# Second-chunk key norms from the diagonal of k k^T instead of from turned tokens, in a one-core hybrid decoder block

## The chip, the cores and the metric

One core of one Trainium2 chip runs the whole program. The metric is device time in microseconds of one execution, lower is better. The kernel is written instruction by instruction for each engine: TensorE (PE), VectorE (DVE), ScalarE (ACT), GpSimd (POOL) and SyncE (SP, which only issues loads and stores).

## The reference, cut to what matters

A decoder block on x (256 tokens, 1024 channels). The input is normalised and projected by `w_in`; a gated DeltaNet branch (8 heads of 128 channels) and an attention branch (8 heads) run on parts of the projection, are gated, projected, merged and projected once more. The change touches the keys of the DeltaNet branch. They pass a causal convolution of four taps and SiLU and are normalised per token:

```python
def l2_normalize(x):
    return x * lax.rsqrt(jnp.sum(x * x, axis=-1, keepdims=True) + NORM_EPS)
...
gdiff = gc[..., :, None] - gc[..., None, :]
decay = jnp.where(tri_incl, jnp.exp(jnp.where(tri_incl, gdiff, 0.0)), 0.0)
lower = jnp.where(tri_strict, jnp.einsum('bhnid,bhnjd->bhnij', kbc, kc) * decay, 0.0)
t_mat = lax.linalg.triangular_solve(eye + lower, jnp.broadcast_to(eye, lower.shape), ...)
```

`g` is a per-token log decay and `gc` its running sum, `beta` (in `kbc`) a sigmoid; both come from 16 extra columns of the projection. The kernel takes chunks of 128 tokens, two per head (c = 0 and 1). What it needs of a token's key norm is the sum of squares over 128 channels, which is also the diagonal element of the product k k^T of that chunk.

## The kernel before, in words

**Tiles and steps.** The weights are read in tiles of 512 KB. The main loop goes over 80 of them (BRANCH0), three steps each: step S = 3n is the first third of tile n, S = 3n+1 the second, S = 3n+2 the last. A float32 product is made from rounded parts: w_hi by h_hi (first third), w_hi by h_lo (second), w_lo by h_hi (third). Every engine walks the same steps S in its own program and adds, at fixed steps, its share of the work beside the tiles; the order on each engine is written out by hand through these step numbers, and semaphores alone tie the engines together. Slots for raw, high and low parts hold 4 tiles (SLOTS); ScalarE makes the high part of tile n+2 (`split_hi`, L634) at the middle step of tile n, VectorE the low part (`split_lo`, L862) at its last step, each behind the other work of the step. SP's loads are held by s_lo: two tiles are loaded when the low part of a tile three before is done (L387).

**The first 16 tiles** are FIRST = "KVKKVKKVKKVKVVVV" (L53). K tiles give the transposed keys of one head each, into bank 0 or 1 (L1282); V tiles give the attention values in two groups of four tiles, which accumulate in two banks each (L1300; bE, bF, then bB, bE). At the end of a group `value_third` makes TensorE wait for its own last product and then adds to s_vg_p (L1306 to L1308), for which ScalarE's copies (`value_front`, L704) wait. The tiles 16 and up follow with gates, then six tiles per head, all in banks 0 and 1.

**A key head.** After K tile of head j, at three, four and six steps behind its first third: ScalarE copies the product with the first tap (L684), VectorE adds the other taps (L936), ScalarE takes tanh (L687), VectorE finishes kT_all (L949, semaphore s_kact). TensorE's `key_tokens` (L1348, steps TOKENS) turns both chunks into bank bD; ScalarE takes the sum of squares of each (L696, s_ksq) and keeps the turned first chunk (L698, s_k0). GpSimd makes the norms of two heads at once (`norms`, L474 to L483, s_sig). `similarity` on TensorE (L1359, steps SIM) makes k k^T of both chunks of head j in bank bA or bC by turns, VectorE's `similarity` (L960) multiplies it at the same step with the norm and the decay E into la_all (s_la). Before, these stand at steps 28 to 44 and the product of head j waits until head j-2 has been taken (L1354).

**Where la_all and E go.** The running sum of g (`gates`, TensorE and VectorE at S = 11, ScalarE at S = 12) is stored to memory by GpSimd as g_rows (L541), loaded back spread over the partitions (L545), masked (L495), and ScalarE takes its exponential at steps 26 to 33 (`decay`, L675). GpSimd stores la_all as blocks (L504) and loads them into `sub` (L513); from S = 58 VectorE solves the triangular systems there (`substitution`).

**The start.** TensorE turns the 8 blocks of normalised x (`turn`, L1199) into seven banks, block 7 inside the first tile (at "lh0", L1257 to L1260). ScalarE makes h_hi of each (L647), VectorE h_lo (L887). Tile 1's low part is made by VectorE in two halves (`first_lo`, L882), then the low part of the 16 gate columns (L893), for which TensorE's gate product waits at S = 4 (L1224). The product for the attention bias (L1237) is made at S = 6 in bank bB and copied by VectorE (L913).

**Banks.** Eight PSUM banks of 512 float32 columns per partition: 0 and 1, then bA to bF for 2 to 7.

```python
FIRST = "KVKKVKKVKKVKVVVV"
TOKENS = {10: 0, 16: 1, 19: 2, 24: 3, 27: 4, 32: 5, 35: 6, 40: 7}
SIM = {28: 0, 29: 1, 30: 2, 31: 3, 36: 4, 37: 5, 43: 6, 44: 7}
```

## Time and profile before

| | |
|---|---|
| median of 3 runs | 368.65 us (368.65 to 368.69) |
| the profiled execution | 368.64 us |
| its span in the trace | 366.9 us |
| TensorE busy | 357.3 us, 97% |
| VectorE busy | 269.6 us, 73% |
| ScalarE busy | 219.1 us, 60% |
| GpSimd busy | 59.7 us, 16% |
| granted TensorE clock, mean | 0.997 of full speed |

The span runs from the first to the last instruction that the profiler recorded; the device time of the same execution is 1.7 us longer. Engines are called PE, DVE, ACT, POOL and SP in the rows, and L12 is line 12 of the kernel before. In rows of a timeline or of the chain the first number is the start in us from the beginning of the span, the second the time taken in us. Rows of a timeline merge neighbouring instructions of one line (x4 is four of them), and in square brackets stands how long the engine had been idle before, and what ended it. A matmul's time in a timeline reaches until its result is out, so that neighbours overlap; the distance from start to start is what it costs the engine. A float32 product of 128 columns has two records, so a similarity of two chunks shows as x4.

### The profile page before, as it was taken

How to read it: one execution, taken by the hardware profiler on the slowest of the kernel's cores; microseconds unless marked ns; L12 is line 12 of the kernel's file. 1: busy time of each engine (PE TensorE's matmuls, PEld its weight loads, DVE VectorE, ACT ScalarE, POOL GpSimd, SP SyncE). 2: the span in 40 equal slices, each digit the busy share in tenths (PEclk: the TensorE clock that was granted, in tenths of full speed). 3: DMA queues.
4: the chain of work that ended last, by engine and by line, in shares of the span. 5: the costliest groups of instructions: out<-in, count | busy, mean ns of one | idle time of the engine just before them, and what ended most of it. 6: DMA issues, size and time to landing. Idle time of an engine off the chain costs nothing.

```text
span 366.9 us, 7653 instructions
## 1 busy us (share of the span) xinstructions
PE 357.3 (97%) x2755; PEld 343.1 (94%) x2755; DVE 269.6 (73%) x559; ACT 219.1 (60%) x500; POOL 59.7 (16%) x119
## 2 busy tenths in 40 slices
PE   7999999999999999999999999999999999999993
PEld 5889987899999999999999999999999999999882
DVE  2968876489976878978788678697885657667644
ACT  5776894455455665767676676667676542533521
POOL 1534341740033001102020202001020100000011
PEclk9999999999999999999999999999999999999998
DMA  8749549788789465544655455554456474874623
GB/s 262 204 150 283 178 124 236 185 236 226 195 198 240 114 181 152 127 117 121 178 148 129 118 134 154 142 147 117 121 151 186 118 220 134 219 230 170 236 110 114
DMA packets 99343, 62.45 MB, mean 170 GB/s; under 512 B 3652, under 2 KB 94190, under 8 KB 99310
## 3 DMA queue, kind: packets, MB, share of 16 engines
q1 hardware_dynamic: 98014, 58.59, 58.1%
q0 software_dynamic: 1296, 3.43, 3.5%
q8 instruction: 20, 0.33, 0.4%
q14 instruction: 13, 0.11, 0.1%
HBM read 60.41 MB, written 1.59 MB: 169 GB/s over the span
## 4 chain that ended last, share of the span: by engine, by line
PE 90%; DVE 3%; ACT 3%; issue 1%; DMA 1%; POOL 0%; DVEq 0%; SPq 0%; ACTq 0%; POOLq 0%
PE banks L1282 67%; PE banks L1499 6%; PE banks L1300 4%; DMA xin<-in_x_dram 1%; PE banks L1382 1%; PE banks L1389 1%; PE banks L1400 1%; ACT h_hi L647 1%; DVE w_lo L862 1%; PE banks L1438 1%; PE banks L1224 1%; PE banks L1441 1%; ACT w_hi L634 1%; DVE acc L936 1%; PE banks L1359 0%
## 5 line engine op out<-in xcount | busy, mean ns | idle before, releaser
L862 DVE TENSOR_TENSOR w_lo<-raw,w_hi 128x1024 fp32r<-128x1024 f32 x102 | 124.1, 1220 | 31.3 <-ACT w_hi L634 31.0
L634 ACT CAST w_hi<-raw 128x1024 fp32r<-128x1024 f32 x103 | 106.8, 1046 | 6.0 <-PE banks L1499 4.5
L1282 PE MATMUL banks<-h_hi,w_hi 128*128 128x256 f32 x568 | 82.3, 287 | 0.6 <-PE banks L1300 0.6
L1282 PE MATMUL banks<-h_hi,w_lo 128*128 128x256 f32 x568 | 82.4, 288 | 0.0
L1282 PE MATMUL banks<-h_lo,w_hi 128*128 128x256 f32 x568 | 82.2, 287 | 0.0
L1282 PEld LDWEIGHTS banks<-h_hi,w_hi 128*128 128x128 f32 x568 | 72.7, 191 | 2.1 <-issue 2.0
L1282 PEld LDWEIGHTS banks<-h_lo,w_hi 128*128 128x128 f32 x568 | 72.7, 191 | 0.0
L1282 PEld LDWEIGHTS banks<-h_hi,w_lo 128*128 128x128 f32 x568 | 72.7, 191 | 0.0
L936 DVE SCALAR_TENSOR_TENSOR acc<-banks,vec,acc 128x255 f32<-128x255 f32 (+2 forms) x72 | 34.5, 479 | 6.2 <-ACT acc L731 3.5
L584 POOL TENSOR_TENSOR so<-so,rnq 128x2 f32<-128x2 f32 x8 | 3.8, 471 | 148.8 <-ACT junk L798 148.8
L842 ACT CAST h_hi<-tacc 128x256 f32 x8 | 3.2, 406 | 28.4 <-DVE tacc L1163 28.4
L739 ACT ACTIVATE tz<-banks 128x256 f32<-128x256 f32 x16 | 6.1, 384 | 22.7 <-PE banks L1282 22.7
L1282 PE MATMUL banks<-y_hi,w_hi 128*128 128x256 f32 x128 | 18.0, 283 | 0.0
L1282 PE MATMUL banks<-y_hi,w_lo 128*128 128x256 f32 x128 | 18.0, 283 | 0.0
L1282 PE MATMUL banks<-y_lo,w_hi 128*128 128x256 f32 x128 | 18.0, 283 | 0.0
L731 ACT ACTIVATE acc<-banks,vec 128x256 f32<-128x256 f32 x16 | 7.6, 474 | 15.0 <-PE banks L1282 14.9
L1282 PEld LDWEIGHTS banks<-y_hi,w_hi 128*128 128x128 f32 x128 | 16.5, 192 | 0.0
L1282 PEld LDWEIGHTS banks<-y_lo,w_hi 128*128 128x128 f32 x128 | 16.5, 192 | 0.0
L1282 PEld LDWEIGHTS banks<-y_hi,w_lo 128*128 128x128 f32 x128 | 16.5, 192 | 0.0
L1499 PE MATMUL banks<-w_hi,h_hi 128*128 128x512 f32 x32 | 12.5, 389 | 0.0
L1499 PE MATMUL banks<-w_lo,h_hi 128*128 128x512 f32 x32 | 12.5, 389 | 0.0
L1499 PE MATMUL banks<-w_hi,h_lo 128*128 128x512 f32 x32 | 12.4, 389 | 0.0
(243 smaller groups left out, 544.4 us busy)
## 6 DMA issues: line engine op xcount, KB each, us to landing
raw<-in_w_in_dram SPq DMA_DIRECT2D x80, 512.0 KB, 5.1
raw<-in_w_branch_dram SPq DMA_DIRECT2D x16, 512.0 KB, 4.8
raw<-in_w_out_dram SPq DMA_DIRECT2D x8, 512.0 KB, 4.1
xin<-in_x_dram SPq DMA_DIRECT2D x2, 512.0 KB, 3.8
th_E<-g_rows POOLq DMA_DIRECT2D x2, 512.0 KB, 7.1
bias<-bias_rows POOLq DMA_DIRECT2D x1, 1024.0 KB, 6.7
raw<-in_x_dram SPq DMA_DIRECT2D x2, 512.0 KB, 3.9
out_dram<-xin SPq DMA_DIRECT2D x4, 256.0 KB, 2.0
```

The lines of the kernel that those rows point to most:

```text
L584: pool.tensor_tensor(so[:, 2:4], so[:, 0:2], rnq[:, g % 2, :], ALU.add).then_inc(s_f, 1)
L634: nc.scalar.copy(w_hi[:, t % SLOTS, :], raw[:, t % SLOTS, :]).then_inc(s_hi, 1)
L647: ac(h_hi[:, k, :], x_T[k], ACT.Copy, scale=vec[:, R_PRE + k:R_PRE + k + 1]).then_inc(s_h_hi, 1)
L731: ac(acc[:, t, :], ps, ACT.Copy, scale=tap(CONV - 1, 2 * t, h)).then_inc(s_tap0, 1)
L739: ac(tz[:, t - 4, :], ps, ACT.Tanh, scale=0.5).then_inc(s_tz, 1)
L862: v.tensor_tensor(w_lo[:, t % SLOTS, cols], raw[:, t % SLOTS, cols], w_hi[:, t % SLOTS, cols].bitcast(F32), ALU.subtract).then_inc(s_lo, 1)
L936: v.scalar_tensor_tensor(out=acc[:, a, i:], in0=ps[:, 0:SEQ - i], scalar=tap(CONV - 1 - i, w, h), in1=acc[:, a, i:], op0=ALU.mult, op1=ALU ...
L1224: last = mm(bA[0:4 * HEADS, 0:SEQ], wbd2[:, k, :], h_part[:, k, :], start=k == 0 and h_part is h_hi, stop=k == KT - 1 and h_part is h_lo)
L1282: last = mm(ps, w, r, start=part == 0 and k == 0, stop=part == 2 and k == KT - 1)
L1300: last = mm(((bE, bF), (bB, bE))[group][c], left, right, start=q == 0 and kk == 0 and part == 0, stop=q == 3 and kk == 1 and part == 2)
L1382: last = mm(bA[:, P * c:P * c + P], kT_all[:, g, P * c:P * c + P], q_T[:, P * c:P * c + P], start=True, stop=True)
L1499: last = mm(bank[2 + 2 * c + e], m[:, k, P * c:P * c + P], w[:, (OUT0 + k) % SLOTS, 512 * e:512 * e + 512], start=k == 0 and m is m_hi and ...
```

## The change

- `key_tokens`: TensorE turns only the first chunk of each head, ScalarE squares only that chunk.
- `similarity` on TensorE moves to steps 14, 16, 19, 24, 30, 32, 35 and 40. Two heads share a bank, the even one in columns 0 to 255, the odd one in columns 256 to 511. An odd head waits until VectorE has read the diagonal of the even one (s_kdiag); heads 4 and 6 wait until the pair that used the bank before has been taken; heads 0 and 2 wait until the running sums have been read from bA (s_gc).
- new on VectorE: `diagonal(j)`, one tensor_tensor_reduce of the second chunk's product with the identity, into ssqk, at the step after the product. GpSimd's `norms` waits for it as well.
- VectorE's multiplication with norm and decay stays where it was, but for heads 6 and 7, which go from steps 43, 44 to 44, 45; it waits for both products of the pair.
- the running sum's steps: 11 to 12 on TensorE and VectorE, 12 to 13 on ScalarE.
- the start: x is turned into six banks, so blocks 6 and 7 are turned inside the first tile; the bias product moves there too, into bank bC; the two small loads that it needs are issued before tile 1's; VectorE makes the gate columns' low part before the second half of tile 1's.
- TensorE no longer waits for its own product at the end of a value group; ScalarE's second copy of a group waits for the tile's semaphore.

```diff
--- before.py
+++ after.py
@@ -68,8 +68,11 @@
 U0, W0, UW_STRIDE = 99, 111, 16
 
 
+
 TOKENS = {10: 0, 16: 1, 19: 2, 24: 3, 27: 4, 32: 5, 35: 6, 40: 7}
-SIM = {28: 0, 29: 1, 30: 2, 31: 3, 36: 4, 37: 5, 43: 6, 44: 7}
+SIM = {14: 0, 16: 1, 19: 2, 24: 3, 30: 4, 32: 5, 35: 6, 40: 7}
+DIAGONAL = {15: 0, 17: 1, 20: 2, 25: 3, 31: 4, 33: 5, 36: 6, 41: 7}
+DECAYED = {28: 0, 29: 1, 30: 2, 31: 3, 36: 4, 37: 5, 44: 6, 45: 7}
 E0 = 26
 PAIRS = BLK // 2
 STEPS = 18
@@ -211,7 +214,7 @@
         tri = cst[:, C_TRI:C_TRI + P]
 
 
-        x_T = [bank[1 + k % 7][:, SEQ * (k // 7):SEQ * (k // 7) + SEQ] for k in range(KT)]
+        x_T = [bank[(1, 2, 3, 5, 6, 7)[k % 6]][:, SEQ * (k // 6):SEQ * (k // 6) + SEQ] for k in range(KT)]
 
         def tap(k, w, h):
 
@@ -281,6 +284,7 @@
         s_k0 = sem("s_k0")
         s_kact = sem("s_kact")
         s_ks_p = sem("s_ks_p")
+        s_kdiag = sem("s_kdiag")
         s_ksq = sem("s_ksq")
         s_kt_p = sem("s_kt_p")
         s_la = sem("s_la")
@@ -399,14 +403,14 @@
                     col = COL_VB + 512 * (i // 4)
                     load(n, n, w_in[256 * (i % 4):256 * (i % 4) + 256, col:col + 512].rearrange("(k p) n -> p k n", p=P))
 
-            for n in range(2):
-                first_load(n)
+            first_load(0)
+            sp.dma_start(hot, onehot).then_inc(s_hot, 16)
+            sp.dma_start(relb[0:BUCKETS, :], rel_bias).then_inc(s_hot, 16)
+            first_load(1)
             sp.dma_start(cst[:, P:], consts[:, P:]).then_inc(s_cst, 16)
             sp.dma_start(wbd[:], w_in[:, COL_BD:COL_B].rearrange("(k p) n -> p k n", p=P)).then_inc(s_bd_w, 16)
             sp.dma_start(alog[:], dn_a_log.rearrange("(a n) -> a n", a=1).to_broadcast([P, HEADS])).then_inc(s_small, 16)
             sp.dma_start(dtb[:], dn_dt_bias.rearrange("(a n) -> a n", a=1).to_broadcast([P, HEADS])).then_inc(s_small, 16)
-            sp.dma_start(hot, onehot).then_inc(s_hot, 16)
-            sp.dma_start(relb[0:BUCKETS, :], rel_bias).then_inc(s_hot, 16)
             for n in range(2, len(FIRST)):
                 first_load(n)
             for g in range(EARLY):
@@ -472,7 +476,8 @@
             def norms(q):
 
                 heads = slice(2 * q, 2 * q + 2)
-                pool.wait_ge(s_ksq, 4 * q + 4)
+                pool.wait_ge(s_ksq, 2 * q + 2)
+                pool.wait_ge(s_kdiag, 2 * q + 2)
                 pool.tensor_scalar(tk[:, 0, :, heads], ssqk[:, :, heads], 0.25, EPS, ALU.mult, ALU.add).then_inc(s_nk, 1)
                 pool.wait_ge(s_nk, 2 * q + 1)
                 pool.tensor_tensor(tk[:, 1, :, heads], tk[:, 0, :, heads], power[:, 1], ALU.pow).then_inc(s_nk, 1)
@@ -663,7 +668,7 @@
                     ac(tiny[:, 16:24], alog[:], ACT.Exp).then_inc(s_ga, 1)
                     sa.wait_ge(s_gs, 1)
                     ac(gt[:, 5], gt[:, 4], ACT.Ln).then_inc(s_ga, 1)
-                elif S == 12:
+                elif S == 13:
                     sa.wait_ge(s_gc, 3)
                     ac(tab[:, 7, :], tab[:, 5, :], ACT.Exp).then_inc(s_tab, 1)
                     ac(tab[:, 8, :], gt[:, 9, 0], ACT.Exp).then_inc(s_tab, 1)
@@ -689,18 +694,18 @@
             def key_tokens(j):
 
                 sa.wait_ge(s_kt_p, j + 1)
-                ps = bD[:, 0:256]
-                for c in range(NC):
-                    if j or c:
-                        sa.wait_ge(s_ksq, 2 * j + c)
-                    ac(junk[:, 0:P], ps[:, P * c:P * c + P], ACT.Square,
-                       accum_out=ssqk[:, c, j:j + 1]).then_inc(s_ksq, 1)
-                nc.scalar.copy(k0_all[:, j, :], ps[:, 0:P]).then_inc(s_k0, 1)
+                if j:
+                    sa.wait_ge(s_ksq, j)
+                ac(junk[:, 0:P], bD[:, 0:P], ACT.Square, accum_out=ssqk[:, 0, j:j + 1]).then_inc(s_ksq, 1)
+                nc.scalar.copy(k0_all[:, j, :], bD[:, 0:P]).then_inc(s_k0, 1)
 
             def value_front(i):
 
                 group, c = i // NC, i % NC
-                sa.wait_ge(s_vg_p, i + 1)
+                if c == 0:
+                    sa.wait_ge(s_vg_p, group + 1)
+                else:
+                    sa.wait_ge(s_tile, V_TILES[4 * group + 3] + 1)
                 nc.scalar.copy(vtok_all[:, c, 512 * group:512 * group + 512],
                                ((bE, bF), (bB, bE))[group][c]).then_inc(s_vtok, 1)
 
@@ -888,10 +893,10 @@
                                        in1=h_hi[:, k, :].bitcast(F32), op0=ALU.mult, op1=ALU.subtract).then_inc(s_h_lo, 1)
             ve.wait_ge(s_lo, 2)
             first_lo(1, 0, s_lo)
-            first_lo(1, 1, s_lo)
             ve.wait_ge(s_bd_hi, 1)
             v.tensor_tensor(wbd2[:, :, 2 * HEADS:], wbd[:], wbd2[:, :, 0:2 * HEADS].bitcast(F32),
                             ALU.subtract).then_inc(s_bd_s, 1)
+            first_lo(1, 1, s_lo)
             v.tensor_scalar(won[:], vec[:, R_ON:R_ON + 1], -0.5, None, ALU.mult).then_inc(s_vec, 1)
             v.tensor_scalar(vec_half[:], vec[:], 0.5, None, ALU.mult).then_inc(s_vec, 1)
             def gates(S):
@@ -910,7 +915,7 @@
                     for c in range(NC):
                         v.tensor_tensor(gt[:, 1, c], bd[:, c, HEADS:], dtb[:], ALU.add).then_inc(s_gv, 1)
                     ve.wait_ge(s_bias_p, 1)
-                    v.tensor_copy(brow, bB[0:HEADS, 0:BIAS_W]).then_inc(s_brow, 1)
+                    v.tensor_copy(brow, bC[0:HEADS, 0:BIAS_W]).then_inc(s_brow, 1)
                 elif S == 9:
 
                     ve.wait_ge(s_ga, 5)
@@ -920,7 +925,7 @@
                     ve.wait_ge(s_gs, 9)
                     ve.wait_ge(s_gv, 4)
                     v.tensor_tensor(tab[:, 9:11, :], gt[:, 5], gt[:, 7], ALU.add).then_inc(s_g, 2)
-                elif S == 11:
+                elif S == 12:
                     ve.wait_ge(s_gc_p, 1)
                     v.tensor_copy(grow[:], bB[0:HEADS, 0:SEQ]).then_inc(s_grow, 1)
                     v.tensor_copy(tab[:, 4:6, :], bA[:, 0:16].rearrange("p (c n) -> p c n", c=NC)).then_inc(s_gc, 1)
@@ -949,14 +954,23 @@
                     v.scalar_tensor_tensor(out=kT_all[:, j, :], in0=tacc[:, a, :], scalar=1.0, in1=acc[:, a, :],
                                            op0=ALU.add, op1=ALU.mult).then_inc(s_kact, 1)
 
+            def diagonal(j):
+
+                ve.wait_ge(s_G_p, j + 1)
+                if j:
+                    ve.wait_ge(s_kdiag, j)
+                ps = (bA, bC)[j // 2 % 2][:, 256 * (j % 2) + P:256 * (j % 2) + 2 * P]
+                v.tensor_tensor_reduce(products[:, 0:P], ps, ident, 1.0, 0.0, ALU.mult, ALU.add,
+                                       ssqk[:, 1, j:j + 1]).then_inc(s_kdiag, 1)
+
             def similarity(j):
 
                 if j % 2 == 0:
                     ve.wait_ge(s_sig, j + 1)
                 ve.wait_ge(s_E, 2 * j + 2)
-                ve.wait_ge(s_G_p, j + 1)
+                ve.wait_ge(s_G_p, j // 2 * 2 + 2)
                 for c in range(NC):
-                    ps = (bA, bC)[j % 2][:, P * c:P * c + P]
+                    ps = (bA, bC)[j // 2 % 2][:, 256 * (j % 2) + P * c:256 * (j % 2) + P * c + P]
                     v.scalar_tensor_tensor(out=la_all[:, j, c, :], in0=ps, scalar=tab[:, c, j:j + 1],
                                            in1=E_all[:, j, c, :], op0=ALU.mult, op1=ALU.mult).then_inc(s_la, 1)
 
@@ -1131,8 +1145,10 @@
                 gates(S)
                 for j in range(HEADS):
                     key_front(j, S - 3 * K_TILES[j] - 3)
-                if S in SIM:
-                    similarity(SIM[S])
+                if S in DIAGONAL:
+                    diagonal(DIAGONAL[S])
+                if S in DECAYED:
+                    similarity(DECAYED[S])
                 for g in range(HEADS):
                     stage_w(g, S - W0 - UW_STRIDE * g)
                     stage_u(g, S - U0 - UW_STRIDE * g)
@@ -1208,8 +1224,8 @@
                 turn(1, k)
             pe.wait_ge(s_pre_x0b, 1)
             pe.wait_ge(s_pre_x[1], 1)
-            for k in range(4, 7):
-                if k == 6:
+            for k in range(4, 6):
+                if k == 5:
                     pe.wait_ge(s_vec, 1)
                 for c in range(NC):
                     turn(c, k)
@@ -1231,11 +1247,7 @@
                         last = tp(bA[:, 256 + 4 * HEADS * c:256 + 4 * HEADS * (c + 1)], bd_T[:, P * c:P * c + P],
                                   ident[0:4 * HEADS, 0:4 * HEADS])
                     last.then_inc(s_bd_p, 1)
-
-                    pe.wait_ge(s_hot, 32)
-                    pe.wait_ge(s_relb, 1)
-                    mm(bB[0:HEADS, 0:BIAS_W], relb[:], hot, start=True, stop=True).then_inc(s_bias_p, 1)
-                elif S == 11:
+                elif S == 12:
 
                     pe.wait_ge(s_g, 2)
                     pe.wait_ge(s_brow, 1)
@@ -1255,9 +1267,13 @@
                 for i, which in enumerate(order):
                     k = int(which[2])
                     if which == "lh0":
-                        pe.wait_ge(s_h_lo, 1)
+                        pe.wait_ge(s_hot, 32)
+                        pe.wait_ge(s_relb, 1)
+                        mm(bC[0:HEADS, 0:BIAS_W], relb[:], hot, start=True, stop=True).then_inc(s_bias_p, 1)
+                    if which in ("lh0", "lh1"):
+                        pe.wait_ge(s_h_lo, k + 1)
                         for c in range(NC):
-                            turn(c, 7)
+                            turn(c, 6 + k)
                     if which[0] == "l":
                         pe.wait_ge(s_h_lo, k + 1)
                     else:
@@ -1303,9 +1319,6 @@
                             last.then_inc(s_vg_p, 1)
                 if part == 2:
                     last.then_inc(s_tile, 1)
-                    if q == 3:
-                        pe.wait_ge(s_tile, n + 1)
-                        pe.sem_inc(s_vg_p, 1)
 
             def bank_free(n):
 
@@ -1344,19 +1357,20 @@
                     pe.wait_ge(s_k0, j)
                 else:
                     pe.wait_ge(s_h_lo, KT)
-                for c in range(NC):
-                    last = tp(bD[:, P * c:P * c + P], kT_all[:, j, P * c:P * c + P], ident)
-                last.then_inc(s_kt_p, 1)
+                tp(bD[:, 0:P], kT_all[:, j, 0:P], ident).then_inc(s_kt_p, 1)
 
             def similarity(j):
 
-                if j >= 2:
-                    pe.wait_ge(s_la, 2 * (j - 1))
+                pe.wait_ge(s_kact, j + 1)
+                if j % 2:
+                    pe.wait_ge(s_kdiag, j)
+                elif j >= 4:
+                    pe.wait_ge(s_la, 2 * (j - 2))
                 else:
                     pe.wait_ge(s_gc, 3)
                 for c in range(NC):
-                    k = kT_all[:, j, P * c:P * c + P]
-                    last = mm((bA, bC)[j % 2][:, P * c:P * c + P], k, k, start=True, stop=True)
+                    k, col = kT_all[:, j, P * c:P * c + P], 256 * (j % 2) + P * c
+                    last = mm((bA, bC)[j // 2 % 2][:, col:col + P], k, k, start=True, stop=True)
                 last.then_inc(s_G_p, 1)
 
             def stage_a(g, s):
```

## Rows read from the trace of the kernel before

**Rows 1.** The page of the profile: busy time by engine, and the chain's shares by engine

```profile
PE 357.3 (97%) x2755; PEld 343.1 (94%) x2755; DVE 269.6 (73%) x559; ACT 219.1 (60%) x500; POOL 59.7 (16%) x119
...
PE 90%; DVE 3%; ACT 3%; issue 1%; DMA 1%; POOL 0%; DVEq 0%; SPq 0%; ACTq 0%; POOLq 0%
```

**Rows 2.** Waits of TensorE, whole span: waited for: us in total, times, longest us

```profile
PE banks L1282 <- PE banks L1300: 0.6, 2, 0.3
...
PE banks L1438 <- DVE sub L1101: 0.4, 1, 0.4
```

**Rows 3.** The chain that ended last, 14 to 112 us: start, us, what

```profile
18.68 0.74 PE banks L1237 x2
...
24.61 0.53 PE banks L1244 x4
...
30.44 0.22 PE banks L1348 x2
...
42.68 0.44 PE banks L1359 x4
...
58.42 2.76 PE banks L1300 x12
...
66.94 45.35 PE banks L1282 x376
```

**Rows 4.** Timeline of VectorE, 24 to 31 us

```profile
24.39 1.51 DVE L936 SCALAR_TENSOR_TENSOR acc<-banks,vec,acc 128x255 f32<-128x255 f32 x3
25.82 0.40 DVE L925 COPY grow<-banks 8x256 f32<-8x256 f32 x1
...
26.49 1.22 DVE L862 TENSOR_TENSOR w_lo<-raw,w_hi 128x1024 fp32r<-128x1024 f32 x1
27.63 0.42 DVE L949 SCALAR_TENSOR_TENSOR kT_all<-tacc,acc 128x256 f32<-128x256 f32 x1
...
30.89 1.23 DVE L862 TENSOR_TENSOR w_lo<-raw,w_hi 128x1024 fp32r<-128x1024 f32 x1
```

**Rows 5.** Timeline of VectorE, 42 to 55 us

```profile
42.05 1.52 DVE L936 SCALAR_TENSOR_TENSOR acc<-banks,vec,acc 128x255 f32<-128x255 f32 x3
...
44.63 0.61 DVE L960 SCALAR_TENSOR_TENSOR xin<-banks,tab,th_E 128x128 f32<-128x128 f32 x2 [0.55 <-PE banks L1359]
...
48.44 0.60 DVE L960 SCALAR_TENSOR_TENSOR xin<-banks,tab,th_E 128x128 f32<-128x128 f32 x2
...
54.05 0.99 DVE L936 SCALAR_TENSOR_TENSOR acc<-banks,vec,acc 128x255 f32<-128x255 f32 x2
```

**Rows 6.** Timeline of TensorE, 48 to 67 us

```profile
48.05 0.38 PE L1348 MATMUL banks<-cst,kT_all 128*128 128x128 f32 x2
...
57.98 0.44 PE L1348 MATMUL banks<-cst,kT_all 128*128 128x128 f32 x2 [0.44 <-DVE kT_all L949]
...
65.57 1.07 PE L1300 MATMUL banks<-w_lo,h_hi 128*128 128x512 f32 x4
```

**Rows 7.** Timeline of TensorE, 10 to 15 us

```profile
10.12 0.44 PE L1199 MATMUL banks<-cst,xin 128*128 128x128 f32 x2
...
14.60 0.30 PE L1224 MATMUL banks<-h_hi,wbd 128*32 128x256 f32 x1 [0.22 <-DVE wbd L893]
```

**Rows 8.** Timeline of ScalarE at 11.5 us: the last block of h_hi

```profile
11.49 0.52 ACT L647 ACTIVATE h_hi<-banks,vec 128x256 fp32r<-128x256 f32 x1
```

**Rows 9.** DMA traffic, 0 to 14 us in 40 slices of 0.35 us each

```profile
GB/s 0 0 0 0 0 234 140 398 421 375 398 445 386 269 315 249 218 307 328 376 357 357 392 386 310 189 77 9 37 54 156 286 323 350 345 347 309 294 288 250
```

**Rows 10.** Timeline of GpSimd at 35 us: both masks of E

```profile
35.33 2.63 POOL L495 TENSOR_SCALAR_AFFINE_SELECT th_E<-th_E 128x1024 f32<-128x1024 f32 x2 [1.46 <-DMA th_E<-g_rows]
```

**Rows 11.** Timeline of ScalarE at 40 us: the first exponentials of E

```profile
40.53 0.70 ACT L675 ACTIVATE th_E<-th_E,ng 128x128 f32<-128x128 f32 x2
```

**Rows 12.** L868 of VectorE: count, ns min/median/max, start, form

```profile
L868 DVE CUSTOM_DVE_ANT_0 bias<-xin x1: 692/692/692, 5.5 to 5.5; 128x512 f32<-128x512 f32 x1
L868 DVE DVE_READ_ACCUMULATOR2_ANT tiny<- x1: 80/80/80, 6.2 to 6.2; 128x1 f32 x1
```

## The prediction

> **What bounds the kernel now.** I read the page first. TensorE is busy 97% of the span and makes up 90% of the chain that ended last [rows 1]. So a microsecond taken off TensorE counts only where TensorE does not then wait for somebody else. The list of waits shows how little it waits: twice 0.3 us for its own matmuls at the end of a value group, and 0.4 us once late in the kernel [rows 2]. Behind 67 us it runs on, 376 matmuls in one piece [rows 3], so the question is when TensorE begins the first third of tile 16 (step S=48), today at 66.94.
>
> Next I read the stage before that in step with VectorE. VectorE works without a pause from 24.39 to past 30.89 [rows 4], and from 42.05 towards the keys of head 7 it has few gaps [rows 5]; TensorE at 57.98 waits for it [rows 6]. In this stage both engines end close together: what TensorE saves is at VectorE's mercy.
>
> **The change, part by part.**
>
> *Removed from TensorE.* Eight transposes: a pair costs 0.22 in the chain [rows 3], so 0.11 each, 0.9 in all. The wait for its own tile: the last value third starts at 65.57 and the next tile at 66.94, 1.37 us apart, while a value third costs 2.76/3 = 0.92 [rows 3, 6]. So 0.45 is lost, there and once more at tile 10. The bias product, 0.74 [rows 3], moves into the first tile, and the wait for the split gate weights (0.22 idle [rows 7]) goes because VectorE makes them half a split earlier. Total at face value: 0.9 + 0.9 + 0.7 + 0.2 = 2.7 us. I expect none of it but the last wait to survive.
>
> *First tile.* The bias product now stands between the products of block 1 and the transposes of block 6. It begins at about the 10.1 at which block 7 is turned today [rows 7]; then 0.74, a pair of turns 0.22, two matmuls at 0.12 (45.35/376 [rows 3]) and the next pair: block 7 is turned by 11.4 and visible to ScalarE about 11.6. ScalarE starts on block 7 at 11.49 today [rows 8]. I charge 0.1 us to ScalarE and to all of VectorE's work behind it. The two small loads overtake tile 1's load on SP's queue: the queue's traffic collapses to 9 GB/s in the slice at about 9.4 us, so everything issued by then, these included, has landed [rows 9], before 10.1. Tile 1's load goes out about 0.7 later and is read only after the h_hi series, so nothing.
>
> *Step 11 to 12.* VectorE's tail order becomes taps, split 5, g rows. The same work is permuted: taps to 24.39 + 1.43 = 25.82, split 1.14 to 26.96, the four small ones 0.67 (25.82 to 26.49) to 27.63 [rows 4]. All behind it stands where it did. POOL's store of g and the two loads of E start 1.1 later; POOL's mask ends at 35.33 + 2.63 = 37.96, ScalarE first reads E at 40.53, so 2.6 us cover it [rows 10, 11].
>
> *Added to VectorE.* Eight diagonals. The trace has no such instruction on 128x128 from PSUM. Lower bound: one product of that shape from PSUM, 0.30 (0.61 for two [rows 5]), and nothing for the sum. Upper bound: the 128x512 multiply-and-sum, 692 + 80 ns = 0.77 [rows 12]. The shape is that of the lower row and the extra read is that of the upper: 0.30 + 0.08, I take 0.38 of VectorE's time and 0.42 until TensorE sees it. ScalarE loses a square and its read per head; its chain is not the one below, so I book nothing. POOL's norms wait for the diagonals too: those of heads 0 to 5 are made 11, 5 and 3 steps before their first use, and the last pair decides only POOL's last store. The step of the two exponentials, the wait for vec one block sooner and ScalarE's waits for the value tiles move waits that are over by then: nothing.
>
> The Trainium skill (VectorE: DVE Perf Modes, "The TRN2 errata") gives 120 + FD cycles at 0.96 GHz for PSUM to SBUF, an estimate of 0.26 us, and its section "Two Vector instructions with no wait between them" says that an accumulator output is a second instruction. The rows of the 128x512 form agree on the second instruction, 80 ns [rows 12]; for the first, 0.30 as against 0.26, the formula would make the sum below 3 x 0.04 = 0.1 us smaller.
>
> *Added waits, the crux.* Similarity j (odd) shares a bank with j-1 and waits for diagonal j-1; the queue of tiles stands behind it.
>
> (a) S=16. The gates' g is a VectorE result and is read at about 24.6 both before and after [rows 3]; all that TensorE gained ahead of it is given back there. Gates' products about 1.1, two value thirds 1.84: TensorE is at similarity 0 at 27.5 and waits until VectorE has read the bank, 27.63 + 0.1 + 0.06 = 27.8. Then 0.44 [rows 3], a value third, a key third 0.96, one transpose: at 30.2 it stands at similarity 1. Diagonal 0 sits behind split 6 and the keys of head 2, so it begins where split 7 begins today, 30.89 [rows 4], plus 0.1, and is visible 0.42 later: similarity 1 starts at 31.45. Stall 1.2. Its tile third then starts at 31.89 against 30.44 + 0.22 = 30.66: 1.23 late.
>
> (b) S=32. Up to tile 8's end come similarities 2 and 3 (0.88) and two fewer transposes (0.22): TensorE 1.9 late. ScalarE copies tile 8's bank when it is done and VectorE's taps, today 42.05, start at 43.95. From there to diagonal 4 it has the work it has today between 42.05 and 48.44, less the 0.6 in which it waited for a similarity: 5.8 [rows 5]. So diagonal 4 starts at 49.75 and releases at 50.2. TensorE would be there at 48.05 + 1.23 - 0.33 (three single transposes instead of pairs) - 0.44 (three similarities since S=16 where there were four) + 0.11 (its transpose): 48.6. Stall 1.5.
>
> (c) S=40. After similarity 5 (0.44): value third 0.92, two key thirds 1.92, transpose and similarity 6 (0.55), key third 0.96: tile 11 ends at 55.0, the taps of head 7 start 0.5 behind, 55.5, against 54.05 [rows 5]. From them to TensorE's start at 57.98 is 3.93 today; diagonal 6 adds 0.38. TensorE gets the keys of head 7 at 59.8, 1.8 late, having waited over a microsecond.
>
> (d) The tail. From 57.98 to 66.94 is 8.96. It loses a transpose 0.11, similarity 6 0.44 (done earlier) and the wait for its own tile 0.45: 7.96. Tile 16 starts at 67.76, **0.8 us later**.
>
> Sum: the profiled execution took 368.64 us (span 366.9), the median of the runs is 368.65, so the two are one number. 368.64 + 0.8 = **369.45**, slower by 0.22%, just over the 0.2% that a measurement of this kernel can tell from no change. Behind 67 us no instruction is added; POOL's last store of blocks comes some 1.5 us later, and the substitution with it, but TensorE's only late wait of 0.4 us [rows 2] shows that this path is off its back. The cover is VectorE's room there; if it is used up, the late products of head 0 wait by what is left.
>
> **Rivals.**
>
> *Faster: VectorE reaches diagonals 0 and 4 in time.* Then (a) and (b) vanish. Place: S=16 and S=32. Point: diagonal 0 would have to be out by 30.2, 1.2 us sooner than 31.4. TensorE would be 2.6 us further on at tile 11, ahead of today, but the taps of head 7 then wait for VectorE's and ScalarE's own work, which is today's: they start near today's 54.05, earlier by what ScalarE's missing square gives, and diagonal 6 takes that back. The keys come at today's 57.98, and with the tail of 7.96 tile 16 starts at 65.94: 1.0 less, **367.65**. For it: VectorE has idle time before 42. Against it: none of it lies in the stretch from 24.39 to 30.89.
>
> *No change.* The stalls are there, but a diagonal costs the lower bound, 0.30, without the read, and the first tile costs ScalarE nothing: three diagonals lie on the chain (0, 4, 6), 3 x 0.1 less, and 0.1: 369.05, 0.1% over today. Within 0.2% too is anything up to 369.38.
>
> *Slower by more.* The diagonal costs the upper bound: 3 x 0.37 more, **370.55**. Or the first tile delays ScalarE by more than 0.1: each tenth comes through whole.
>
> *Not what it says: TensorE's wait at the value groups stays in another form*, since tile 16's bank or its weights hold it: 0.45 on the tail, 369.9. Against it: the list has that wait twice only, behind tiles 10 and 15 [rows 2].
>
> The change's own wait cannot be a matter of chance: the Trainium skill (PSUM — Partial Sum Buffer, "PSUM bank collisions raise a hardware error") says that a write by TensorE and a read by VectorE in one bank collide even at different columns. No row here shows such an overlap; without the wait the time would be the first rival's.
>
> **How the numbers follow.** Forecast with its own spread (369.4 to 369.9): 0.45. No change by cheap diagonals or by VectorE a few tenths ahead: 0.33. Faster: 0.12. Dearer diagonals or a late first tile: 0.10. Slower by over 0.2% takes the last and, with the wait that stays, nearly all of the first: 0.54; within 0.2% 0.34; faster 0.12. The range 367.9 to 370.5 takes in all but the full first rival and the far end of the upper bound.
>
> **What the profile after would show.** TensorE idle at similarity 1 (about 1.2 us, near 31) and at similarity 5 (about 1.4, near 50), both released by VectorE's new line, about 1.2 us at the last key transpose, near 59; no idle at tile 16, which starts near 67.7; diagonals of 0.30 plus a read of 0.08. Wrong if similarity 1 starts without a wait, if a diagonal takes over 0.6, or if the start of tile 16 and the end differ in their shift.

## The result, and the profile after

| | before, same chips | after |
|---|---|---|
| median of the runs | 368.69 us (6 runs, 368.65 to 369.06) | 372.28 us (6 runs, 371.64 to 372.77) |
| ratio | 1 | 1.0095 [1.0084, 1.0105] |
| profiled execution | 368.64 us | 372.37 us |
| its span | 366.9 us | 370.6 us |
| granted TensorE clock, mean | 0.997 | 0.995 |

The change costs 3.6 us where 0.8 was forecast, and the time lies outside the range given. The clock has no part in it: 0.995 as against 0.997 of full speed, the higher of the two levels (2.4 GHz) in both.

I read the page first, the line of busy times and the chain's shares, columns as in [rows 1].

```profile
PE 356.9 (96%) x2747; PEld 342.1 (92%) x2747; DVE 271.2 (73%) x575; ACT 216.9 (59%) x484; POOL 60.3 (16%) x119
...
PE 74%; DVE 12%; DMA 6%; issue 4%; ACT 2%; POOL 2%; DVEq 0%; SPq 0%; POOLq 0%; ACTq 0%
```

TensorE is busy 0.4 us less than before and the program takes 3.7 us more. Its share of the chain falls from 90% to 74%, and transfers, which had 1%, now have 6%. So the end is now set in part by a way that leads through transfers and VectorE. The list of TensorE's waits (us in total, times, longest) says what stops it:

```profile
PE banks L1373 <- DVE ssqk L963: 1.7, 2, 0.9
PE banks L1298 <- DVE acc L941: 1.5, 1, 1.5
...
PE banks L1360 <- DVE kT_all L954: 1.0, 1, 1.0
PE banks L1298 <- DVE w_lo L867: 0.5, 1, 0.5
```

The first line is the similarities' wait for the diagonals (two of them), the third the wait for the keys of head 7: both forecast. The second and the fourth were not, and the wait of the value groups in [rows 2] is gone.

**Up to tile 16.** TensorE between 30 and 69 us (start, us, idle before in brackets):

```profile
30.59 0.27 PE L1360 MATMUL banks<-cst,kT_all 128*128 128x128 f32 x1
31.62 0.68 PE L1373 MATMUL banks<-kT_all 128*128 128x128 f32 x4 [0.76 <-DVE ssqk L963]
...
47.07 0.68 PE L1373 MATMUL banks<-kT_all 128*128 128x128 f32 x4 [0.27 <-DVE xin L974]
...
49.45 0.27 PE L1360 MATMUL banks<-cst,kT_all 128*128 128x128 f32 x1
50.63 0.68 PE L1373 MATMUL banks<-kT_all 128*128 128x128 f32 x4 [0.92 <-DVE ssqk L963]
...
60.37 0.33 PE L1360 MATMUL banks<-cst,kT_all 128*128 128x128 f32 x1 [1.05 <-DVE kT_all L954]
...
67.36 1.07 PE L1316 MATMUL banks<-w_lo,h_hi 128*128 128x512 f32 x4
68.27 1.11 PE L1298 MATMUL banks<-h_hi,w_hi 128*128 128x256 f32 x8
```

Similarity 1 starts at 31.62 and similarity 5 at 50.63 (forecast 31.45 and 50.2), head 7's keys are turned at 60.37 (59.8), and tile 16 follows its forerunner by 0.91 us without an idle moment, at 68.27 instead of 66.94 [rows 3]: **1.33 us late**, where I had 0.82. VectorE's diagonal is two instructions, as expected:

```profile
31.19 0.28 DVE L963 CUSTOM_DVE_ANT_0 sub<-banks,cst 128x128 f32<-128x128 f32 x1
31.40 0.08 DVE L963 DVE_READ_ACCUMULATOR2_ANT ssqk<- 128x1 f32 x1
```

0.28 and 0.08, where I took 0.30 and 0.08. The estimate of 0.26 worked out from the Trainium skill (VectorE: DVE Perf Modes, "The TRN2 errata") is 0.02 under the row, and the second instruction is there, as the Trainium skill's section "Two Vector instructions with no wait between them" on the same page says.

**Behind tile 16.** The span is 3.7 us longer and tile 16 only 1.33 late: the other 2.4 us are lost behind 67 us, where the change adds no instruction. The chain that ended last (start, us, what), followed back from the stop of TensorE at 110.97, shows by which way:

```profile
64.39 0.33 DVE xin L974
64.72 1.05 DVE w_lo L867
65.77 0.61 DVE xin L974 x2
...
66.94 0.65 POOL m_blocks L509
...
68.76 5.35 DMA m_blocks<-xin
...
74.39 0.48 POOL sub L518
74.87 6.54 DMA sub<-m_blocks
...
81.56 0.10 DVE sub L989
...
83.95 1.22 DVE w_lo L867
...
102.48 4.67 DMA raw<-in_w_in_dram
107.17 1.06 ACT w_hi L639
...
110.97 5.06 PE banks L1298 x40
```

Read from the top: VectorE's decay product of head 6, a low part of weights, the product of head 7, GpSimd's store of the blocks, its landing, the load of `sub`, its landing, and the substitution. There VectorE stands still with its weight work queued behind. The same three places in the timelines of VectorE and GpSimd, first before, then after:

```profile
64.28 2.40 POOL L504 DMA_DIRECT2D m_blocks<-xin  x4 [3.10 <-DVE xin L960]
...
70.24 0.97 POOL L513 DMA_DIRECT2D sub<-m_blocks  x2 [2.56 <-DMA m_blocks<-xin]
...
75.61 0.09 DVE L975 MEMSET sub<- 128x32 f32 x1
```

```profile
66.94 2.41 POOL L509 DMA_DIRECT2D m_blocks<-xin  x4 [2.59 <-DVE xin L974]
...
74.39 0.97 POOL L518 DMA_DIRECT2D sub<-m_blocks  x2 [4.03 <-DMA m_blocks<-xin]
...
81.56 0.09 DVE L989 MEMSET sub<- 128x32 f32 x1 [4.67 <-DMA sub<-m_blocks]
```

The store goes out 2.66 us later, the load 4.15 later, the substitution starts 5.95 later, and 4.67 of that VectorE spends idle.

Part of the 2.66 lies in the norms of heads 6 and 7, for which VectorE's product of head 6 waits (it starts at 64.11), and which now wait for the diagonal of head 7. GpSimd's first instruction of these norms, before and after:

```profile
59.31 0.19 POOL L476 TENSOR_SCALAR tk<-ssqk 128x4 f32<-128x4 f32 x1 [4.27 <-ACT junk L696]
```

```profile
61.65 1.02 POOL L481 TENSOR_SCALAR tk<-ssqk 128x4 f32<-128x4 f32 x1 [3.31 <-DVE ssqk L963]
```

It is not only later but takes 0.8 us longer, beside a low part that VectorE makes from 61.40 to 62.62, and it lies on the chain. No run isolates these 0.8 us.

From 66 to 126 us the list of waits then shows ScalarE, which splits the weights, short of them; before, that wait was 0.4 us in all:

```profile
ACT w_hi L639 <- DMA raw<-in_w_in_dram: 14.5, 9, 3.2
```

SP may load two tiles only when a low part is done, the low parts stand behind the idle VectorE, so the loads come late in a row. TensorE uses up its lead and stops before 85.22 (0.48 us) and 110.97 (1.49 us). Its weight loads, listed apart from its matmuls, wait 0.7 and 1.7 us at these two places, together the 2.4.

### The profile page after: what moved, and what is told of

Read it like the earlier page. It is cut to its first block, busy times and chain, and to the rows that moved or that the text cites. A ratio compares the mean times of both kernels' runs of the same rounds, so it can differ in the third digit from the quotient of the medians.

```text
span 370.6 us, 7651 instructions
## 1 busy us (share of the span) xinstructions
PE 356.9 (96%) x2747; PEld 342.1 (92%) x2747; DVE 271.2 (73%) x575; ACT 216.9 (59%) x484; POOL 60.3 (16%) x119
## 4 chain that ended last, share of the span: by engine, by line
PE 74%; DVE 12%; DMA 6%; issue 4%; ACT 2%; POOL 2%; DVEq 0%; SPq 0%; POOLq 0%; ACTq 0%
PE banks L1298 54%; PE banks L1513 6%; DVE w_lo L867 5%; DVE acc L941 2%; DMA sub<-m_blocks 2%; DVE sub L1014 1%; DMA m_blocks<-xin 1%; DMA raw<-in_w_in_dram 1%; DMA xin<-in_x_dram 1%; PE banks L1316 1%; PE banks L1396 1%; PE banks L1403 1%; PE banks L1414 1%; DVE xin L974 1%; PE banks L1373 1%
```

## The experiments

The question was how the 3.6 us divide between the stage before tile 16 and the way of the blocks behind it, which edit pays for each, and which part was lost in a third way. Each expectation names its theories in its own words. Edits are against the kernel before (the `before` diffs) or the changed kernel (`after`).

**Late blocks alone, in the kernel before.** VectorE's product of head 7 goes from step 44 to 48, TensorE's stays.

```diff
--- before
+DVE_SIM = {28: 0, 29: 1, 30: 2, 31: 3, 36: 4, 37: 5, 43: 6, 48: 7}
...
-                if S in SIM:
-                    similarity(SIM[S])
+                if S in DVE_SIM:
+                    similarity(DVE_SIM[S])
```

> The kernel before with one multiplication of VectorE (norm and decay of head 7) moved from step 44 to step 48, nothing else. Theory 1 (the second half of the loss is the blocks' way: la of head 7, GpSimd's last store of blocks, its load, VectorE's substitution, the weight splits queued behind it): the last store is issued some 2.4 us later (near 66.7 instead of 64.28), VectorE waits for the blocks at step 58 for 3 to 5 us, TensorE's tile 16 still starts at 66.94, and the kernel loses 1.5 to 2.5 us: 370.2 to 371.2. Theory 2 (the loss behind tile 16 has another cause, such as the loads of E or the norms being late): within 0.3 us of before, 368.4 to 369.0.

Measured: 368.82 us, ratio 1.0001 [0.9992, 1.0011]: nothing. The run missed its own condition: VectorE reaches step 48 early, so the store went out at 65.76, only 1.48 later. What it does show is that a delay of this size is free; the substitution started at 76.51 after 0.84 us of idle VectorE, and nobody felt it.

**Later blocks, in the kernel before.** The same with step 50, and behind ScalarE's copy of the last values.

```diff
--- before
+DVE_SIM = {28: 0, 29: 1, 30: 2, 31: 3, 36: 4, 37: 5, 43: 6, 50: 7}
...
+                if j == 7:
+                    ve.wait_ge(s_vtok, 4)
```

> The kernel before with VectorE's multiplication for head 7 at step 50 and behind ScalarE's last copy of the values, so that GpSimd's last store of blocks goes out near 68.3 us, 4 us later than before and 1.4 us later than in the changed kernel. Theory 1 (the blocks' way costs nothing up to a threshold between the 1.5 us of the run with step 48 and the changed kernel's 2.7, and then everything): VectorE waits over 3 us at the substitution with a weight split behind it, the loads of weights come late, TensorE waits for splits or taps, and the kernel loses 1 to 3 us, 369.8 to 371.8, though TensorE starts tile 16 at 66.9. Theory 2 (lateness of the blocks is harmless and the changed kernel lost behind tile 16 by something else): 368.4 to 369.2.

Measured: 370.09 us, ratio 1.0036 [1.0022, 1.0049]. The store went out at 69.04, 4.76 later than before and later than meant; it landed fast (a median of 1.9 us), so that the substitution starts only 3.94 later, 2.0 earlier than in the changed kernel. The timeline of VectorE has, with the changed kernel's signature:

```profile
79.55 0.09 DVE L978 MEMSET sub<- 128x32 f32 x1 [3.60 <-DMA sub<-m_blocks]
```

and its list of waits, 66 to 126 us:

```profile
ACT w_hi L635 <- DMA raw<-in_w_in_dram: 12.7, 10, 2.7
...
PE banks L1285 <- DVE acc L937: 0.8, 1, 0.8
```

Its profiled execution took 370.34 us, 1.7 over that of before: 0.3 arose before tile 16 (67.25), 1.4 behind it. So late blocks cost time by themselves, without one diagonal in the kernel, though not the whole 2.4 us, since they come less late.

**The decay products of heads 6 and 7 at their old steps.**

```diff
--- after
-DECAYED = {28: 0, 29: 1, 30: 2, 31: 3, 36: 4, 37: 5, 44: 6, 45: 7}
+DECAYED = {28: 0, 29: 1, 30: 2, 31: 3, 36: 4, 37: 5, 43: 6, 44: 7}
```

> The changed kernel with the decay products of heads 6 and 7 at steps 43 and 44 as before, so that no weight split stands between them. Theory 1: the last store of blocks goes out 1.1 us earlier (near 65.8), the wait at the substitution shrinks by 1 to 3 us, tile 16 stays at 68.3, and 0.5 to 2 us come back: 370.3 to 371.8. Theory 2: unchanged, 372.0 to 372.6.

Measured: 369.92 us (369.85 to 370.02), ratio 1.0032 [1.0020, 1.0044]: **2.4 us back from two step numbers**, more than the first theory gave (370.3 at best). VectorE and GpSimd:

```profile
64.12 1.13 DVE L974 SCALAR_TENSOR_TENSOR xin<-banks,tab,th_E 128x128 f32<-128x128 f32 x4 [1.49 <-POOL tab L485]
...
76.89 0.09 DVE L989 MEMSET sub<- 128x32 f32 x1
```

```profile
65.81 2.40 POOL L509 DMA_DIRECT2D m_blocks<-xin  x4 [1.46 <-DVE xin L974]
...
71.66 0.97 POOL L518 DMA_DIRECT2D sub<-m_blocks  x2 [2.44 <-DMA m_blocks<-xin]
```

Without the split of weights between the two products (they ran at 64.11 and 65.77) the store is 1.13 us earlier, but the load is 2.73 earlier and the substitution 4.67. Tile 16 starts at 68.28, as in the changed kernel, and TensorE has no wait at all between 66 and 126 us. What is left, 369.92 against 368.73 before, is 1.2 us: tile 16's 1.33.

**The substitution five steps later.** If VectorE's idle stand at 81.56 is the harm, putting the substitution where its data are there should avert it.

```diff
--- after
-SUB_AT = [58, 59, 59, 61, 62, 64, 65, 67, 68, 70, 73, 73, 74, 76, 77, 79, 81, 82]
+SUB_AT = [s + 5 for s in [58, 59, 59, 61, 62, 64, 65, 67, 68, 70, 73, 73, 74, 76, 77, 79, 81, 82]]
```

> The changed kernel with all 18 steps of VectorE's substitution five steps later, nothing else. Theory 1: the blocks come as late as in the changed kernel, but VectorE no longer stands at them with the weight splits behind it; the two late waits of TensorE (0.5 us for a split, 1.5 us for the taps) go, tile 16 stays at 68.3, so 370.2 to 370.4, 1.9 us under the changed kernel. Theory 2 (the substitution's end is what counts, through the loads of the solved blocks for step 99): the same as the changed kernel or slower, 372 to 374.

Measured: 373.5 us (373.26 to 374.93), 1.2 over the changed kernel. The substitution starts at 82.70 without idling, but the solved blocks are stored at 109.33 instead of 107.13 (before 101.66), and TensorE waits for them:

```profile
PE banks L1431 <- issue: 2.3, 1, 2.3
```

The list names no releaser. By the program this product waits for VectorE's turn of the blocks that GpSimd has loaded back, and VectorE's timeline has it just before TensorE goes on at 123.18:

```profile
122.64 0.45 DVE L1086 STREAM_TRANSPOSE sub<-T_all 128x256 f32<-128x256 f32 x1 [3.72 <-DMA T_all<-t_blocks]
```

The blocks' way has a deadline at its far end too, as the second theory had it. Moving the wait did not help; bringing the blocks earlier, in the run with the old steps, did.

**Diagonals 0 and 4 one step earlier.** The first then stands ahead of the weight split of step 14, the other ahead of a tap and two decay products.

```diff
--- after
-DIAGONAL = {15: 0, 17: 1, 20: 2, 25: 3, 31: 4, 33: 5, 36: 6, 41: 7}
+DIAGONAL = {14: 0, 17: 1, 20: 2, 25: 3, 30: 4, 33: 5, 36: 6, 41: 7}
```

> The changed kernel with two of VectorE's diagonals one step earlier: head 0 at step 14, ahead of the low part of tile 6, and head 4 at step 30, ahead of the decay product of head 2. Theory 1 (the waits of TensorE for diagonals 0 and 4 make the loss before tile 16): both waits fall under 0.3 us, the keys of head 7 come about 1.5 us earlier, tile 16 starts at 66.5 to 66.9, GpSimd's last store is issued about 1.5 us earlier, and the kernel comes to 368.2 to 369.6. Theory 2 (VectorE is the bound anyway and gives the time back elsewhere): tile 16 stays within 0.5 us of 68.3 and the time above 371.3.

Measured: 370.14 us, ratio 1.0034 [1.0020, 1.0048], and a wide spread, 368.38 to 371.0. The time is above the first theory's range, tile 16 within it. The diagonals come at 29.83 and 48.38, the first before TensorE asks, the second just as it does (read by 48.67, similarity 5 starts at 48.82); the list shows no similarity waiting for one. TensorE at similarity 1:

```profile
30.69 0.27 PE L1360 MATMUL banks<-cst,kT_all 128*128 128x128 f32 x1
30.80 0.61 PE L1373 MATMUL banks<-kT_all 128*128 128x128 f32 x4
```

Tile 16 starts at 66.76, 1.5 us earlier: that is what the two stalls, 1.7 us in the list of waits, were worth. The wait for head 7's keys is still there, 1.3 us.

**The bias product back at step 6**, into bC.

```diff
--- after
+                    pe.wait_ge(s_hot, 32)
+                    pe.wait_ge(s_relb, 1)
+                    mm(bC[0:HEADS, 0:BIAS_W], relb[:], hot, start=True, stop=True).then_inc(s_bias_p, 1)
...
                     if which == "lh0":
-                        pe.wait_ge(s_hot, 32)
-                        pe.wait_ge(s_relb, 1)
-                        mm(bC[0:HEADS, 0:BIAS_W], relb[:], hot, start=True, stop=True).then_inc(s_bias_p, 1)
```

> The changed kernel with the bias product back at step 6, into bank bC, out of the first tile. Theory 1 (the bias product between the turns of the first tile holds up ScalarE's h_hi and with it everything of VectorE by 0.3 us): h_hi of block 7 ends 0.35 us earlier, VectorE's chain and tile 16 follow by 0.3, and the time falls by 0.3 to 0.6 us, 371.7 to 372.0. Rival (the product costs TensorE its 0.74 us on the path at step 6): the time rises by up to 0.7 us.

Measured: 371.8 us (370.28 to 372.61), ratio 1.0074 [1.0051, 1.0096]; tile 16 at 68.06, 0.21 earlier. ScalarE's series of h_hi, first after, then here:

```profile
8.97 3.36 ACT L652 ACTIVATE h_hi<-banks,vec 128x256 fp32r<-128x256 f32 x8 [0.30 <-PE banks L1215]
```

```profile
9.08 3.03 ACT L652 ACTIVATE h_hi<-banks,vec 128x256 fp32r<-128x256 f32 x8 [0.31 <-PE banks L1215]
```

The bias product in the first tile makes the series 0.33 us longer. In this execution the series started 0.11 later, so it ends 0.22 earlier, at 12.11 instead of 12.33, and tile 16 starts 0.21 earlier: what the end of the series gains reaches tile 16 whole. The intervals of this run and of the changed kernel overlap, so of the time itself I say no more.

**TensorE no longer waits for its own tile, in the kernel before.** This part of the change alone.

```diff
--- before
-                sa.wait_ge(s_vg_p, i + 1)
+                if c == 0:
+                    sa.wait_ge(s_vg_p, group + 1)
+                else:
+                    sa.wait_ge(s_tile, V_TILES[4 * group + 3] + 1)
...
-                    if q == 3:
-                        pe.wait_ge(s_tile, n + 1)
-                        pe.sem_inc(s_vg_p, 1)
```

> The kernel before with TensorE's wait for its own last product at the end of both value groups taken out (ScalarE's second copy waits for the tile). Theory 1: the one at tile 15 is worth its 0.45 us and the one at tile 10 is given back at the keys of head 7: 368.2 to 368.3, 0.12% less. Rival (both count): 367.8. Rival (neither): 368.7.

Measured: 368.26 us (11 runs), ratio 0.9988 [0.9979, 0.9997]. TensorE:

```profile
57.98 0.44 PE L1348 MATMUL banks<-cst,kT_all 128*128 128x128 f32 x2 [0.97 <-DVE kT_all L952]
...
66.48 1.12 PE L1285 MATMUL banks<-h_hi,w_hi 128*128 128x256 f32 x8
```

The first of the two waits is handed back whole: the keys of head 7 come at 57.98 as before, and the wait for them grows from 0.44 [rows 6] to 0.97. The second counts: tile 16 at 66.48 instead of 66.94, and the time falls by as much.

**The changed kernel mended**, first with all three edits (early diagonals, bias product at step 6, decay products at their old steps), then without the bias product's. The diffs are those above.

> The changed kernel with three edits: the two diagonals one step earlier, the bias product at step 6, the decay products of heads 6 and 7 at steps 43 and 44. Theory 1: tile 16 starts near 66.5, the last store goes out at 63.4 to 64.3, no wait of TensorE behind tile 16 is new, 368.0 to 368.4 and with little spread, 0.1 to 0.2% under the kernel before. Rival (the change's own work for VectorE is what costs): above 368.7.

> The changed kernel with diagonals 0 and 4 one step earlier and the decay products of heads 6 and 7 at their old steps; the bias product stays in the first tile. Theory 1 (the first tile's bias product costs the 0.3 us by which it delays ScalarE and VectorE, and nothing gives that back before tile 16): 0.2 us over the version with all three edits, so 368.5 us (368.3 to 368.8), tile 16 near 67.0, no waits for a diagonal, store at 64.9, memset near 76 without a wait. Theory 2 (with the diagonals early, VectorE has the room to take the 0.3 us back, so the place of the bias product is free): the same as with all three edits, 368.3 us, tile 16 at 66.8.

Measured: 368.28 us (11 runs, 368.08 to 368.95), ratio 0.9987 [0.9978, 0.9996], with three; 368.27 us (11 runs, 368.17 to 368.86), ratio 0.9989 [0.9980, 0.9998], with two. The change's whole loss is gone with two lines of step numbers. Once the diagonals are early the bias product's place makes no difference to the time, as the second theory of the last run had it. The trace with three edits is of a slower execution (368.73 us, tile 16 at 67.14 where 66.5 was expected), so the two are compared by their times. TensorE in the last run, the keys of head 7 and tile 16:

```profile
58.61 0.33 PE L1360 MATMUL banks<-cst,kT_all 128*128 128x128 f32 x1 [1.35 <-DVE kT_all L954]
...
66.50 1.12 PE L1298 MATMUL banks<-h_hi,w_hi 128*128 128x256 f32 x8
```

And it is no better than the kernel before with nothing but TensorE's wait on itself gone, 368.26. The rest of the change earns nothing even so: its eight transposes and the moved bias product end in a wait of 1.35 us for the keys of head 7.

**All kernels side by side.** Times from the profiled executions; the last column is the span less the start of tile 16.

| kernel | tile 16 | substitution starts | VectorE's idle before it | rest |
|---|---|---|---|---|
| before | 66.94 | 75.61 | 0 | 300.0 |
| before, head 7's product at step 48 | 66.97 | 76.51 | 0.84 | 299.9 |
| before, the same at step 50 | 67.25 | 79.55 | 3.60 | 301.4 |
| before, no wait on itself | 66.48 | 75.09 | 0 | 299.8 |
| after | 68.27 | 81.56 | 4.67 | 302.3 |
| after, bias product at step 6 | 68.06 | 81.03 | 4.34 | 301.6 |
| after, early diagonals | 66.76 | 77.78 | 2.40 | 299.8 |
| after, old steps of heads 6 and 7 | 68.28 | 76.89 | 0 | 299.8 |
| after, three edits (an execution of 368.73 us) | 67.14 | 75.74 | 0 | 299.8 |
| after, two edits | 66.50 | 75.11 | 0 | 300.1 |
| after, substitution 5 steps later | 68.34 | 82.70 | 0 | 303.4 |

The start of tile 16 compares to some 0.3 us only: ScalarE's series of h_hi itself begins between 8.82 (before without the wait, after with two edits) and 9.17 (before with step 50). The rest is 299.8 to 300.1 us in every kernel whose substitution starts by 78, and longer beyond. Up to 2.4 us of idle VectorE are absorbed; at 3.60, 4.34 and 4.67 the price is 1.4, 1.6 and 2.3, so what exceeds the 2.4 comes through nearly one for one. The kernel with early diagonals stands on the edge: its profiled execution was the fastest of its runs (368.38), its median is 1.8 us longer. Its other runs have no trace, so that these fell over the edge is argued from the table, not shown.

## Why the prediction failed

**What held.** The direction, and the crux (a) to (d). VectorE's read costs what was taken (0.28 + 0.08 for 0.30 + 0.08). Diagonal 0 stood behind a weight split and the keys of head 2 and stalled similarity 1 till 31.62 (31.45 forecast); diagonal 4 let similarity 5 go at 50.63 (50.2); the keys of head 7 took the rest (60.37 for 59.8), with a wait of 1.05 us where "over a microsecond" was forecast. The tail is 7.90 us (7.96). The two experiments on the parts confirm the reason: early diagonals give 1.5 us back at tile 16, and the transposes are worth nothing even then. The stalls themselves were shorter than the 1.2 and 1.5 us of (a) and (b): from the transpose's end by starts (30.59 and 49.45, each + 0.11) they are 0.9 and 1.1, since TensorE came later than the forecast 30.2 and 48.6, which does not change when it is released.

What did not hold is a sign that the prediction had named itself: the start of tile 16 and the end differ in their shift, 1.33 and 3.7 us.

**The first tile** was charged 0.1 and cost 0.3: VectorE's kT_all of head 0 started at 19.00 instead of 18.68, and ScalarE's series grew to 3.36 from the 3.03 that the run with the bias product at step 6 has again. I had compared the time at which block 7 is turned with the time at which ScalarE reaches it, and left out block 6, which is turned there too: its turns end at 10.92 + 0.44 = 11.36, while ScalarE, at 0.38 a block, is ready for it at about 11.1 [rows 8], so the series had its delay before block 7. This is the rival "the first tile delays ScalarE by more than 0.1: each tenth comes through whole". The experiment bears it out: 0.22 at the end of the series are 0.21 at tile 16. With 0.33 in place of 0.1 the 0.82 become 1.05; the other 0.3 came in small pieces between 31 and 60 us, among them a wait of similarity 4 for the decay product of its bank (0.27), which I had not booked.

**The step that failed** is the last one of the sum: "Behind 67 us no instruction is added; POOL's last store of blocks comes some 1.5 us later, and the substitution with it, but TensorE's only late wait of 0.4 us shows that this path is off its back." Three things were wrong in it.

1. *The 1.5 us.* The store came 2.66 us later. I passed over the step of heads 6 and 7 as an order that hides: GpSimd's norms end at 64.16 + 0.20, VectorE's two products then need 1.13 us in one piece, but at steps 44 and 45 there is a weight split of 1.05 us of path between them. That the move costs something was to be read in the code: the last decay product is the only thing the store waits for (in the timeline of before above, L960 is the releaser). With the old steps the store is 1.53 late (65.81 for 64.28), so the 1.5 fits a kernel without this move; up to 0.8 of it is the longer first instruction of the norms, which was not in the forecast.
2. *"With it."* A store and a load follow. Both stretch: the last of the four stores lands after 5.35 us as against 3.9 before (median of the four 4.3 as against 1.9), so the load issued in its wake moves by 4.15, and the last load lands after 6.54 as against 4.0. The data come 6.7 us later; 0.7 of that was room. A delay of 2.66 at the store is one of 5.95 at the substitution.
3. *The cover.* TensorE's waits say nothing of how near it is. "The cover is VectorE's room there; if it is used up, the late products of head 0 wait by what is left": this was the right place, never costed. The room was some 2.4 us of idle VectorE, and a delay of 5.95 went over it.

So the missed term is 2.4 us, which the sum had at nothing, and all of it hangs on two step numbers: the run with only these undone measures it, and the kernel before with nothing but late blocks shows the same path at 1.4 us. With the measured 1.33 at tile 16 and that term the sum is 368.64 + 1.33 + 2.4 = 372.4, as the profiled execution has it (372.37).

**The rivals.** *Faster* put 1.0 us on early diagonals, tile 16 at 65.94. With them the start is 66.50 to 66.76: the diagonals do come in time, but the keys of head 7 come at 58.61 rather than "at today's 57.98", since VectorE's diagonals and ScalarE's exponentials in front of them remain (of the chain from 40 to 70 us the exponentials make up 14.3% with two edits, 4.2% before). *No change* and the dearer diagonal fell with the 0.28 + 0.08; the late first tile, of *slower by more*, came true, but with 0.2 us of the 2.8 that were missing. *TensorE's wait in another form* fell with the 0.91 from the last value third to tile 16.

## What to carry to other kernels

An engine's short list of waits tells where it stopped, not how close the others are to stopping it. When a change moves a step past a weight split, follow its result along every hop (store, landing, load, landing, first reader) to the queue that it stands in, and ask how late that queue may start; here 2.4 us of idling were free and 3.6 were not. Put short instructions on which another engine waits ahead of the long ones of their step: four entries of two tables, each moved by one step, were worth all of the 3.6 us.

## What was not expected of the hardware

**A store's landing depends on what it meets.** The four stores of blocks, 32 KB each, by GpSimd's queue, 60 to 90 us, before, after, and with two edits (KB, median us from issue to landing):

```profile
m_blocks<-xin POOLq DMA_DIRECT2D x4, 32.0 KB, 1.9
```

```profile
m_blocks<-xin POOLq DMA_DIRECT2D x4, 32.0 KB, 4.3
```

```profile
m_blocks<-xin POOLq DMA_DIRECT2D x4, 32.0 KB, 2.5
```

The same bytes took 1.9 to 4.3 us by when they were issued. The DMA traffic by slices of 0.75 us shows what they meet: before, it is between 0 and 92 GB/s from 63.7 to 67.5 us, in which they are issued; after, the hole (60 to 144) lies from 67.5 to 69.7, and from there to 73.5 the weight loads move 294 to 350 GB/s. That the weights' traffic holds the stores up fits this. Two more kernels bear it out: with stores issued from 65.76 (before, step 48) into traffic of 303 to 343 GB/s from 66.75 to 70.5 the median is 4.2 us; issued from 65.81 (after, old steps), with traffic down at 87 to 184 GB/s from 67.5 to 69.75, it is 2.5. No run changes the traffic alone.

**Repeatability often falls near a threshold.** The kernel before varies by about 0.4 us from run to run, the kernel with early diagonals by 2.6 and the changed kernel by 1.1; with the blocks back in time (369.92, 368.27) it is 0.2 and 0.7. It is no sure sign: the kernel before with step 50 has late blocks that cost it 1.4 us and varies by 0.5 only.

**VectorE stands still beside GpSimd.** One kT_all in eight takes three times as long, in both kernels. Before, on VectorE:

```profile
35.69 1.31 DVE L949 SCALAR_TENSOR_TENSOR kT_all<-tacc,acc 128x256 f32<-128x256 f32 x1
```

The usual time is 0.42 [rows 4]. GpSimd's two masks run beside it from 35.33 to 37.96 [rows 10]; one takes 1.39 us, the other, which starts at 36.9, 1.09. So the first ends at 36.73, and kT_all at 37.00, 0.27 later; after, 37.16 + 1.43 = 38.59 and 38.87. It looks as if VectorE did not begin before the mask was through. The Trainium skill (SBUF — State Buffer, "Who interferes with whom") says that VectorE with two SBUF inputs and GpSimd reading SBUF share a pair of ports under an exclusive lock, so that the second to issue waits until the first is done; the rows agree. Both kernels pay this one, so it explains nothing of the difference. The same seems to go the other way at the norms of heads 6 and 7: GpSimd's first instruction there, issued at 61.65 into VectorE's low part, ends at 62.67, 0.05 after the low part's 62.62. That one stands on the chain of the changed kernel; before, it ran at 59.31, when no low part was being made.
